# Units of a skinny product moved from the stages between dense streams into the streams

## The reference, cut to what matters

```
h   = x + mix(rmsnorm(x)) @ w_out ; h = h + relu(rmsnorm(h) @ w_up)**2 @ w_down   # first block
mod = silu(c) @ w_mod + b_mod ; mod_c = silu(c_ctx) @ w_mod + b_mod               # w_mod: 2048 x 12288
sh1, sc1, gt1, sh2, sc2, gt2 = split(mod, 6)
z   = (rmsnorm(x) * (1 + sc1) + sh1) @ w_in_2     # and the same for ctx, with mod_c
x   = x + gt1 * (heads(z) @ w_out_2)              # GLA and mLSTM recurrences in two directions
x   = x + gt2 * conv_ffn(rmsnorm(x) * (1 + sc2) + sh2)
```

## Time and profile before

| what | value |
|---|---|
| median of 3 runs | 2802.85 us (2800.95 to 2803.17) |
| the profiled execution | 2801.47 us, span 2799.7 us |
| PE busy | 2628.4 us (94%) |
| DVE, ACT, POOL busy | 1483.8, 1081.7, 40.9 us |
| mean granted TensorE clock | 0.965 of 2.4 GHz |
| read from memory | 525 MB, 188 GB/s over the span |
| chain that ended last | PE 88%, DVE 5%, DMA 3% |
| of that: DMA of w_mod tiles; PE L475 | 3%; 2% |
| one split of a tile: DVE L1289, ACT L967 | 1.219 us, 1.051 us (mean) |
| a dense tile from issue to landing | 3.2 to 3.3 us (median) |
| dense matmuls, start to start, at the full clock | 0.227 us (512 columns) |

### The profile page before, as it was taken

The page is one execution under the profiler, slowest core; times in us unless marked ns, Lnnn a source line. Parts: engine busy times, 40 slices in busy tenths (PEclk is TensorE's granted clock), DMA queues, the critical chain, the costliest instruction groups (busy, mean ns, idle before and its releaser), DMA issues.

```text
span 2799.7 us, 39040 instructions
## 1 busy us (share of the span) xinstructions
PE 2628.4 (94%) x16120; PEld 2254.8 (81%) x16120; DVE 1483.8 (53%) x1836; ACT 1081.7 (39%) x1294; POOL 40.9 (1%) x18
## 2 busy tenths in 40 slices
PE   6999898999999999999799996787989999999997
PEld 4886577989889899778578884556889979998996
DVE  4433435544545545553354436436577766775675
ACT  4433324433434344453344333303433343334333
POOL 0000000000000000000000003200000000000000
PEclk9999998999999999999899998887999999999999
DMA  7552766555555556455545555544535555555554
GB/s 285 192 193 111 295 238 228 183 189 185 187 185 185 188 183 234 151 188 188 214 139 191 192 195 213 190 181 145 186 129 184 183 187 197 183 185 185 184 177 132
DMA packets 143883, 529.17 MB, mean 189 GB/s; under 512 B 16112, under 2 KB 16112, under 8 KB 142464
## 3 DMA queue, kind: packets, MB, share of 16 engines
q1 hardware_dynamic: 143744, 527.17, 54.2%
HBM read 525.01 MB, written 2.10 MB: 188 GB/s over the span
## 4 chain that ended last, share of the span: by engine, by line
PE 88%; DVE 5%; DMA 3%; ACT 2%; issue 1%; SPq 0%; DVEq 0%; ACTq 0%
PE PSA L461 26%; PE PSA L462 26%; PE PSA L463 26%; DMA raw<-in_w_mod 3%; PE PSA L475 2%; PE PSA L801 1%; DVE cv L1267 1%; PE PSA L893 1%; DVE wlo L1289 1%; DVE tpv L1374 1%; PE PSA L582 1%; DMA raw<-in_w_in 1%; ACT whi L967 1%; PE PSA L619 1%; PE PSA L631 0%
## 5 line engine op out<-in xcount | busy, mean ns | idle before, releaser
L1289 DVE TENSOR_TENSOR wlo<-raw,whi 128x1024 fp32r<-128x1024 f32 x788 | 925.5, 1219 | 529.1 <-ACT whi L967 526.4
L967 ACT ACTIVATE whi<-raw 128x1024 fp32r<-128x1024 f32 x788 | 795.2, 1051 | 550.8 <-DMA raw<-in_w_down 209.1
L461 PE MATMUL PSA<-uhi,whi 128*128 128x256 f32 x2400 | 681.8, 284 | 3.2 <-issue 2.8
L462 PE MATMUL PSA<-ulo,whi 128*128 128x256 f32 x2400 | 681.3, 284 | 0.0
L463 PE MATMUL PSA<-uhi,wlo 128*128 128x256 f32 x2400 | 681.3, 284 | 0.0
L461 PEld LDWEIGHTS PSA<-uhi,whi 128*128 128x128 f32 x2400 | 463.0, 193 | 4.6 <-issue 3.4
L462 PEld LDWEIGHTS PSA<-ulo,whi 128*128 128x128 f32 x2400 | 463.0, 193 | 0.2
L463 PEld LDWEIGHTS PSA<-uhi,wlo 128*128 128x128 f32 x2400 | 463.0, 193 | 0.0
L461 PE MATMUL PSA<-whi,uhi 128*128 128x512 f32 x1088 | 432.9, 398 | 27.4 <-DVE wlo L1289 15.5
L462 PE MATMUL PSA<-wlo,uhi 128*128 128x512 f32 x1088 | 430.2, 395 | 0.0
L463 PE MATMUL PSA<-whi,ulo 128*128 128x512 f32 x1088 | 429.7, 395 | 0.0
(11 more groups left out here) (254 smaller groups left out, 1418.8 us busy)
## 6 DMA issues: line engine op xcount, KB each, us to landing
raw<-in_w_up SPq DMA_DIRECT2D x300, 512.0 KB, 3.3
raw<-in_w_in SPq DMA_DIRECT2D x208, 512.0 KB, 3.2
raw<-in_w_mod SPq DMA_DIRECT2D x192, 512.0 KB, 7.1
raw<-in_w_down SPq DMA_DIRECT2D x192, 512.0 KB, 3.2
raw<-in_w_out SPq DMA_DIRECT2D x64, 512.0 KB, 3.2
raw<-in_w_down2b SPq DMA_DIRECT2D x20, 512.0 KB, 3.7
h<-in_x SPq DMA_DIRECT2D x2, 1024.0 KB, 6.2
xc<-in_ctx SPq DMA_DIRECT2D x2, 1024.0 KB, 9.1
```

The lines of the kernel that those rows point to most:

```text
L461: pe.matmul(dst, xh, wh, start=start, stop=False)
L462: pe.matmul(dst, xh, wl, start=False, stop=False)
L967: AF(whi[:, n % SLOTS, 0:w], raw[:, n % SLOTS, 0:w], ACT.Copy).then_inc(hi_done, 1)
L1289: TT(wlo[:, n % SLOTS, 0:w], raw[:, n % SLOTS, 0:w], whi[:, n % SLOTS, 0:w], ALU.subtract).then_inc(lo_done, 1)
```

## The change

The fills are taken out of the list, but for two units in the context states, and a stream can carry units: `units_from` says from which iteration of its loop. There each block has one unit; its four tiles stand one each behind the first four dense tiles, so that such a block has 12 tiles in the ring. The column pass stands behind the sixth dense tile (t = 5). ACT's and DVE's parts stand behind their split of the eighth. All these units use PSUM bank 4. The plan of the new kernel:

```
@@ plan()
-    ph = [Fill("fill_start", (4, 6)), Phase("in1", "tok", 4, 2, 8, k=KD, evac="z1"), Fill("fill_mix", (0, 1, 2, 3) * 2 + (0, 1)),
-          Phase("out1", "tok", 2, 2, 8, k=KD, evac="res"), Fill("fill_mlp", (4, 6) * 3 + (4,))]
+    ph = [Phase("in1", "tok", 4, 2, 8, k=KD, evac="z1"), Phase("out1", "tok", 2, 2, 8, k=KD, evac="res", units_from=0)]
...
-    ph.append(Fill("fill_states", (4, 5, 4, 5, 4, 6, 4)))
-    ph.append(Phase("inL", "tok", 6, 2, 8, k=KD, evac="zl"))
-    ph.append(Fill("fill_heads", (4, 5) * 6 + (4,) + (6, 7) * 3 + (6,) + (4, 6)))
+    ph.append(Fill("states", 2))
+    ph.append(Phase("inL", "tok", 6, 2, 8, k=KD, evac="zl", units_from=1))
@@ SyncE, stream: a unit's tile is issued behind each of the first four
-                            tile(src, p, i, b * p.per_block + t)
+                            tile(src, p, i, p.main_at(i, b, t))
+                            if p.has_unit(i) and t < UNIT:
+                                tile(t_in["w_mod"][UNIT * p.unit_no(i, b) + t], p, i, p.unit_at(b, t))
@@ TensorE, stream: behind the matmuls of tile t
+                            if p.has_unit(i):
+                                if t == 0:
+                                    if not isinstance(i, int) or p.unit_no(i, b):
+                                        pe.wait_ge(mini_done, p.unit_no(i, b))
...
+                                if t < UNIT:
+                                    q = p.unit_at(b, t)
+                                    mod_tile(4, q % SLOTS, p.plus_tiles(16 * (q // SLOTS + 1), i, 2), t)
+                                if t == UNIT + 1:
+                                    mod_columns(4, p.unit_no(i, b))
@@ TensorE, attention heads
-                if 5 <= s < 10:
...
-                    mod_units(BY["fill_mix"], (2 * s - 10, 2 * s - 9), fresh=s == 5)
@@ TensorE, mLSTM loop
-                if 1 <= s < 8:
-                    mod_units(BY["fill_heads"], (GLA_UNITS + s - 1,), fresh=s == 1)
@@ ScalarE and VectorE, stream: behind the split of the eighth tile
+                            if p.has_unit(i) and t == p.per_block - 1:
+                                mod_rows(4, p.unit_no(i, b), p.plus_tiles(p.unit_at(b, UNIT - 1) + 1, i))
+                            if p.has_unit(i) and t == p.per_block - 1:
+                                mod_adds(4, p.unit_no(i, b))
```

More of the change, by code:

```diff
@@ L40 @@
 GROUPS1 = 4
-GLA_UNITS = 13
-Y_UNIT = 20
 UNIT = 4
@@ L78, in __init__ @@
         self.per_iter = self.per_block * blocks
-class Fill:
[L84 to L90, removed]
+        self.units_from = iters if units_from is None else units_from
+        self.units = (iters - self.units_from) * blocks
+        self.unit_tiles = UNIT * blocks if self.units else 0
@@ new lines, in __init__, with has_unit, plus_tiles, main_at @@
+        assert iters == 1 or self.per_iter % SLOTS == 0 and self.unit_tiles % SLOTS == 0
+    def has_unit(self, i):
+        return self.units > 0 and (not isinstance(i, int) or i >= self.units_from)
+    def plus_tiles(self, n, i, times=1):
+        if isinstance(i, int):
+            return n + times * (i * self.per_iter + max(0, i - self.units_from) * self.unit_tiles)
+        return n - times * self.units_from * self.unit_tiles + i * (times * (self.per_iter + self.unit_tiles))
+    def main_at(self, i, b, t):
+        if self.has_unit(i):
+            return self.seq0 + b * (self.per_block + UNIT) + t + min(t, UNIT)
+        return self.seq0 + b * self.per_block + t
@@ L126, in plan @@
         p.main0, p.blk0 = mains, blk
-        seq += p.per_iter * p.iters
+        units += p.units
+        seq += p.plus_tiles(0, p.iters)
         mains += p.per_iter * p.iters
@@ L463, in product, with mod_tile, mod_columns, fill_tiles @@
                 return pe.matmul(dst, xl, wh, start=False, stop=stop)
[L465 to L469, removed]
+            def mod_tile(bank, slot, n, t):
+                pe.wait_ge(arrived[slot], n)
+                for j in range(4):
+                    k = UNIT * t + j
+                    mm = pe.matmul(PSA[32 * j:32 * j + 32, bank, 0:UW], cst[:, 2 * k:2 * k + 32], raw[:, slot, j * UW:(j + 1) * UW],
+                                   start=t == 0, stop=t == UNIT - 1)
+                mm.then_inc(tile_used, 1)
+            def mod_columns(bank, g):
+                pe.wait_ge(row_done, g + 1)
+                for c in range(2):
+                    mm = pe.matmul(PSA[:, bank, UW + 2 * c:UW + 2 * c + 2], modrow[:, c * P:(c + 1) * P], cA("sel"), start=True, stop=True)
+                mm.then_inc(mini_ready, 1)
+            def fill_tiles(f, u, bank):
                 for t in range(UNIT):
                     q = f.seq0 + UNIT * u + t
[L472 to L491, removed]
+                    mod_tile(bank, q % SLOTS, 16 * (q // SLOTS + 1), t)
             def narrow(x, part):
@@ L731, in _ @@
             mm.then_inc(B["suf_ready"], 1)
-            mod_units(BY["fill_states"], range(3), fresh=True)
+            states = BY["states"]
+            pe.wait_ge(mini_done, states.unit0)
+            fill_tiles(states, 0, 4)
+            fill_tiles(states, 1, 5)
+            mod_columns(4, states.unit0)
             pe.wait_ge(B["mr_rev"], 1)
@@ L1101, in context_states @@
                     AF(KE[:, n, :], PSA[:, n, :], ACT.Exp).then_inc(B["suf_exp"], 1)
-                mod_rows(BY["fill_states"], (0, 1))
+                for u in range(2):
+                    mod_rows(4 + u, BY["states"].unit0 + u, BY["states"].seq0 + UNIT * (u + 1))
                 act.wait_ge(B["w_arg"], 1)
                 AF(rows[:, 5, :], rows[:, 4, :], ACT.Exp, bias=mctx[:, 1:2]).then_inc(B["mr_exp"], 1)
-                mod_rows(BY["fill_states"], (2,))
                 for n in range(4):
@@ L1656, in _ @@
                 if p.name == "in1":
-                    first = {p.lead - 1: lambda: (transposes_lo(0, v_("g_mix"), None), mod_adds(BY["fill_start"], range(2)))}
+                    first = {p.lead - 1: lambda: transposes_lo(0, v_("g_mix"), None)}
                 elif p.name == "up1_0":
```

162 lines of the change are left out of this document (60 added, 102 removed).

## The result

The changed kernel takes 2835.39 us (median of 4 runs, 2833.93 to 2839.79) against 2802.51 us for the kernel before in the same comparison (4 runs, 2800.95 to 2803.17): ratio 1.0121, 95% interval 1.0103 to 1.0138. It is slower by 33 us; 2827 was forecast, with 2796 to 2857 as the range. Its profiled execution has a span of 2838.0 us at a mean granted clock of 0.969 (before 2799.7 and 0.965).

A forecast was written before the change was run, and what follows sets the result against it. PE was taken to bound the streams (685.5 of 686 us busy), while stages wait. Units in streams cost 128.8 us, stages give back 104.8: +24.0 on 2801.5, plus 1.4 to the median, 2827 us, range 2796 to 2857.

The forecast's parts named there:

- A unit in a stream, 2.80 us: Each unit moved into a PE-bound stream costs 2.80 us; 46 units cost 128.8 us (115 to 154).
- the insertion: Changing from dense matmuls to a unit's and back, five times a unit, costs 0.08 us each, 0.40 a unit.
- No overlap in the streams, and DVE not late: In the streams no unit cost is hidden, and transfers, ring and DVE's splits beside it add nothing.
- Start, attention, norm, context states: Stages without their units give back 5.7 us (start), 31 (attention heads), 26.5 (norm before up1) and 17.1 (context states).
- the last term: In the context states, ACT splits inL's first tiles earlier, no longer waiting for two unit rows: about 4.5 us.
- GLA levels, 0 us: Removing 13 units from the GLA levels gives back 0 us (-2 to +7); levels stay at 5.3 to 5.5 us.
- Between and behind the GLA directions, -3.5 us: Two units' worth of PE gives 3.5 us; a lower clock in the state's products takes 7 (0 to 12).
- mLSTM, 28 us: Seven mLSTM turns without units give 36.1 us at full clock, less 8 for the clock: 28 us (0 to 36).
- A unit is cheaper in a stream: Rival: column-pass loads hide under dense matmuls in streams, a unit costs 2.06 us, total 2793 us; chance 0.14.
- The clock stays low in the thinned heads: Rival: mLSTM turns at 1.2 GHz take about 10 us, its 28 us are gone, total 2855 us; chance 0.16.
- DVE late: Rival: DVE is late in the streams by 1.2 us in each of 46 blocks, total 2883 us; chance 0.05.
- the stages don't empty: Rival: waits removed before out1 and up1 are half taken by others, total 2856 us; chance 0.07.

The follow-up runs named there:

- the test above: Changed kernel with the four float32 matmuls of each stream unit tile given a constant 128-column stationary operand, one after another: 3009.64 us.
- one place a block: Changed kernel with a unit's four tiles together behind the block's fourth dense tile, not one behind each of the first four: 2789.43 us, ratio 0.9955.

## Why the prediction was right, and where it was off

The sign and its reason were right: the units left stages in which they were partly covered and went into streams in which PE has no idle time, and what they cost there exceeds what the stages gave back. The size came out 8.4 us low, from two errors of opposite sign: the units in the streams cost 33.2 us more than forecast, and the stages gave back 19.4 more. That the total came so close is in part luck. (The two leave 13.8; the two profiled executions lie 5.4 us further apart than the medians.)

- *A unit in a stream, 2.80 us: too low, outside its own bounds.* 162 us against 115 to 154. The column pass was near (0.54 taken, 0.46 measured). The mis-sized term is the insertion: 0.08 us each for five, where each of the four tiles costs 0.34. A unit is 4 x 0.43 for the matmuls, 4 x 0.34 for the places and 0.46 for the pass, 3.54 us; the 1.86 taken for the matmuls already held 0.14 of one such place. The bounds came from the earlier trace rows: transposes (0.02), which have operands of 128 columns, and L512 (0.19). The lower one fits the test above, where 128 float32 columns cost no more than 0.02. But neither row has the unit's form, float32 with 32 columns, so neither bounded it, and the third edge, the long step behind the first dense matmul, was not looked for. "No unit stands inside a stream before" was the place to widen the upper end. (The rounded product of 32 columns in inC did stand in one, and would have shown 0.)
- *No overlap in the streams, and DVE not late:* right. PE is busy 686.00 of 686; the idle time in front of dense rows that waits for DVE is 15.0 + 3.6 us over all of the kernel (15.5 + 3.6 on the page of the kernel before), by these rows of its page (busy us, mean ns, idle before them and what ended most of it):

```profile
L479 PE MATMUL PSA<-whi,uhi 128*128 128x512 f32 x1088 | 442.6, 407 | 20.1 <-DVE wlo L1275 15.0
...
L479 PE MATMUL PSA<-whi,ahi 128*128 128x512 f32 x856 | 344.5, 402 | 3.6 <-DVE wlo L1275 3.6
```

- *Start, attention, norm, context states:* 80.3 forecast, 79.7 measured. Following DVE's and ACT's own chains to what is late next gave these to about 2 us each. The start missed by 2.1: in this execution DVE's normalisation ends at 19.62, where the earlier trace rows have 17.05; with one place a block it ends at 17.12 again. (In the context states the rows give 4.2 for the last term, not 4.5.)
- *GLA levels, 0 us:* 6.2 us came back (the first six levels take 31.1 us instead of the 33.7 of before, the next six 30.7 instead of 34.3), inside the -2 to +7 that was given. The heart of the forecast stood: 13 units are nearly free there. Putting them back costs 12.3 us in the heads and takes 12 x 3.52 = 42 from the streams.
- *Between and behind the GLA directions, -3.5 us:* wrong in sign, and outside the -8.5 to +3.5 that its parts allow. The step between the directions takes 18.3 us instead of 20.7, and from the last level to mLSTM 3.2 us came back, so +5.6 in all. The step that failed is the 7 us taken off for a lower clock in the products of the state: these (L849 to L851) take 10.5 us, from 1861.19 to 1871.66, where they took 12.2 before.
- *mLSTM, 28 us:* from the first L880 to the squaring behind the loop (L1151, at 1940.87) 32.5 us came back. The turns, two rows of the changed kernel's PE timeline:

```profile
1903.19 1.12 PE L880 MATMUL PSA<-rows,ca 8*128 8x512 f32 x2
1908.88 1.12 PE L880 MATMUL PSA<-rows,ca 8*128 8x512 f32 x2
```

  A turn takes 5.69 us (5.5 worked out at the full clock). Of the 8 us taken off for the clock, half wasn't spent.

*The rivals.* "A unit is cheaper in a stream" was wrong by the traces: it wanted under 2.28 us. Only the way into a column pass is free; the pass itself still costs 0.46 us, not 0.1. "The clock stays low in the thinned heads" needs two readings. In the columns of the earlier trace rows, first two stretches of the changed kernel, the first six GLA levels and five mLSTM turns, then the first six levels of the kernel before:

```profile
1771.20:1802.30 31.10, 20.32 (x96) 18.69 (x96) 23.75 (x17) 11.57 (x12) 17.11 (x6) 0.63 0.00 1
1897.50:1926.00 28.50, 27.61 (x132) 20.29 (x131) 18.55 (x55) 3.15 (x5) 0.00 (x0) 1.00 0.00 1
...
1689.10:1722.80 33.70, 28.73 (x309) 21.18 (x309) 23.24 (x22) 13.33 (x18) 17.48 (x6) 0.92 0.83 314
```

In mLSTM, where the rival had it, the clock did not stay low: five turns in a row ran at the full clock. (Over the whole loop it is 0.86, from 1884.3 to 1940.8, against 0.79 from 1814.1 to 1903.1 before.) In the GLA levels it fell, from 0.92 to 0.63, but there the PE rows at the lower level lie mostly where DVE is waited for in any case. GLA's scores in the changed kernel:

```profile
1771.21 3.78 PE L811 MATMUL PSA<-qE,kE 128*128 128x128 f32 x16 [4.92 <-DVE qE L1521]
...
1781.42 2.05 PE L811 MATMUL PSA<-qE,kE 128*128 128x128 f32 x16 [1.32 <-DVE qE L1521]
```

They take 3.78 us at the lower level where the earlier trace rows have 2.02, and the pair of levels still takes 10.2 instead of 10.58, since both rows wait for DVE's L1521. "DVE late" and "the stages don't empty" are refuted by the two points above.

## What to carry to other kernels

Work that moves into a stream bound by PE pays its matmuls in full, and pays for each change between these forms of matmul: count the places, not only the instructions, and put small foreign matmuls together in one place. When a price for an operation is bounded by neighbours, match type *and* operand width; a transpose was no stand-in for a 32-column product. A stage in which another engine sets the pace is a place for spare work: leave there what fits beneath it (13 units at 0.94 us each instead of 2.5 to 3.5), and take out only what is waited for.

## What the runs showed of the hardware that was not expected

- Going from dense matmuls in the rounded type to float32 matmuls with 32 or 64 stationary columns and back costs 0.34 to 0.36 us of PE: 0.09 ahead, about 0.14 in the last matmul of the group (0.57 less 0.43), 0.11 behind the first dense one. The weight loads then start with their matmul instead of one row ahead. With float32 and 128 columns the same costs 0.02 at most, with the rounded type and 32 columns nothing that can be seen. Why it takes both, and which operand's type counts, is open.
- PE counts as busy through these gaps (686.00 of 686): the busy share doesn't show them, only the distance between starts does.
- Four float32 matmuls side by side in groups of 32 columns take 0.43 us, as long as one of 256 columns; one after another they take 1.7 us.
